# Expert stage of a two-block transformer: one-hot blocks one tile later, gate loads apart, gathered dots spread over the routings

## The reference

```python
s = jnp.einsum('chpd,hpnd->chpn', q, keys)
sv, si = lax.top_k(s, K)
cand = sv[:, :, 0, :, None] + sv[:, :, 1, None, :]
cidx = si[:, :, 0, :, None] * N_KEYS + si[:, :, 1, None, :]
top_s, sel = lax.top_k(cand.reshape(C, PEER_HEADS, K * K), K)
eidx = jnp.take_along_axis(cidx.reshape(...), sel, axis=-1)
g = jax.nn.softmax(top_s, axis=-1)
act = jax.nn.gelu(jnp.einsum('chkd,cd->chk', u_tab[eidx], xb), approximate=False)
return jnp.einsum('chk,chkd->cd', g * act, v_tab[eidx])
```

## Time and profile before

| | us |
|---|---|
| median of 3 runs (3055.06 to 3059.49) | 3056.42 |
| the profiled execution | 3056.66 |
| its span, first to last instruction | 3054.9 |
| TensorE busy in the span | 2918.0 |
| VectorE busy | 1802.1 |
| ScalarE busy | 996.8 |
| GpSimd busy | 999.0 |
| first pass, from the first product to the last gelu's end | 380.5 to 1068.4 |
| second pass, first to last product | 1068.4 to 1651.5 |

### The profile page before, as it was taken

One profiled execution on the slowest core, in us unless ns is written; L12 is line 12 of the kernel. 1 busy time (PEld: TensorE's weight loads), 2 busy tenths in 40 slices (PEclk: granted clock), 3 DMA queues, 4 the chain that ended last, 5 costly groups with the idle time before them and its releaser, 6 DMA issues. The chain is left out here.

```text
span 3054.9 us, 39382 instructions
## 1 busy us (share of the span) xinstructions
PE 2918.0 (96%) x15042; PEld 2591.1 (85%) x15042; DVE 1802.1 (59%) x3227; ACT 996.8 (33%) x1582; POOL 999.0 (33%) x611
## 2 busy tenths in 40 slices
PE   8887999999999799999999999999999899999998
PEld 7554799999999799999998787888788898778886
DVE  6785777888887677887884843331143455333311
ACT  4345233443434222222223223222223456332212
POOL 3201500111112432433332544444432344454442
PEclk9767999999999899999999999999999789999999
DMA  3101256786959988999983232233331000223332
GB/s 130 34 1 42 95 145 206 225 277 200 296 179 308 385 294 304 329 324 329 331 305 113 90 104 83 97 97 102 98 130 31 4 1 15 76 83 97 97 103 70
DMA packets 195745, 475.83 MB, mean 156 GB/s; under 512 B 17205, under 2 KB 104117, under 8 KB 193253
## 3 DMA queue, kind: packets, MB, share of 16 engines
q1 hardware_dynamic: 167764, 370.54, 37.0%
q0 software_dynamic: 27648, 100.68, 9.5%
q10 hardware_dynamic: 144, 2.10, 0.2%
HBM read 415.47 MB, written 56.62 MB: 155 GB/s over the span
## 5 line engine op out<-in xcount | busy, mean ns | idle before, releaser
L262 ACT ACTIVATE w_hi<-w 128x1024 fp32r<-128x1024 f32 (+2 forms) x485 | 506.6, 1046 | 1236.3 <-DVE ffn_gates L2119 324.4
L272 POOL TENSOR_TENSOR w_lo<-w,w_hi 128x1024 fp32r<-128x1024 f32 (+2 forms) x229 | 542.4, 2379 | 693.6 <-ACT w_hi L262 693.6
L272 DVE TENSOR_TENSOR w_lo<-w,w_hi 128x1024 fp32r<-128x1024 f32 x256 | 313.5, 1225 | 190.7 <-ACT w_hi L262 158.5
L307 PE MATMUL peer_psum<-xn_hi,w_hi 128*128 128x416 f32 x1024 | 369.0, 360 | 16.2 <-ACT peer_act_out L1627 16.2
L308 PE MATMUL peer_psum<-xn_lo,w_hi 128*128 128x416 f32 x1024 | 363.2, 355 | 0.0
L309 PE MATMUL peer_psum<-xn_hi,w_lo 128*128 128x416 f32 x1024 | 362.7, 354 | 0.0
L307 PE MATMUL peer_psum<-peer_w_hi,w_hi 128*128 128x416 f32 x1024 | 359.8, 351 | 2.1 <-DVE peer_w_lo L404 1.4
L308 PE MATMUL peer_psum<-peer_w_lo,w_hi 128*128 128x416 f32 x1024 | 358.9, 350 | 0.0
L309 PE MATMUL peer_psum<-peer_w_hi,w_lo 128*128 128x416 f32 x1024 | 358.9, 350 | 0.0
L1463 POOL DMA_INDIRECT peer_gathered<-in_peer_u,peer_chosen_here x96 | 141.5, 1474 | 623.0 <-DVEq L1710 496.0
L307 PE MATMUL ffn_psum<-ffn_hn_hi,w_hi 128*128 128x512 f32 x704 | 275.8, 392 | 10.4 <-DVE ffn_hn_lo L617 6.6
(11 more groups left out here) (417 smaller groups left out, 5724.5 us busy)
## 6 DMA issues: line engine op xcount, KB each, us to landing
w<-in_peer_uT SPq DMA_DIRECT2D x128, 512.0 KB
w<-in_peer_v SPq DMA_DIRECT2D x128, 512.0 KB
w<-in_f_w_gu SPq DMA_DIRECT2D x88, 512.0 KB
peer_act<-peer_act_out SPq DMA_DIRECT2D x128, 208.0 KB
peer_gate<-peer_gates_out SPq DMA_DIRECT2D x26, 1024.0 KB, 8.1
peer_gates<-peer_gate SPq DMA_DIRECT2D x16, 1664.0 KB, 9.6
peer_act_in<-peer_act SPq DMA_DIRECT2D x128, 208.0 KB
w<-in_f_w_down SPq DMA_DIRECT2D x32, 512.0 KB
```

Of the source, the lines that this page charges most:

```text
L262: act.activation(self.hi[:, x, 0:c], self.buf[:, x, 0:c], ACT.Copy).then_inc(self.rounded, 1)
L272: eng.tensor_tensor(self.lo[:, x, 0:c], self.buf[:, x, 0:c], self.hi[:, x, 0:c].bitcast(F32), ALU.subtract).then_inc(self.split, 1)
L307: pe.matmul(out, w[0], x[0], start=start, stop=False)
```

## The change

Five edits, all in `peer`:

- `block_tile` names the tile one later, so TensorE multiplies each block's one-hot matrices, ACT copies the gates out and SP stores them one tile later than before.
- SP loads the gates of q = 0 at c = 120 (`NK - 8`) instead of c = 122, still behind a wait for all gate stores. The gates of q = 1 are loaded behind the gelu of tile n = 4 in the second pass, not at c = 122.
- The tail makes one dot per tile.
- Each of the routings 1, 2 and 3 makes two dots, at two places in its chain.
- `EARLY` is 68: 48 in the blocks, 6 in the routings, 14 in the tail. So 28 dots are left to the second pass (20 before); `SHARES` goes from 23 to 31, and the adding of `peer_v` rows runs over n = 32 to 127 instead of 24 to 119.

```diff
-EARLY = 76
+EARLY = 68
@@
-                block_tile[START[r] + TURN + 1 + i] = b
+                block_tile[START[r] + TURN + 2 + i] = b
@@
-                    if c == NK - 6:
+                    if c == NK - 8:
                         for i in range(2):
                             sp.wait_ge(g_stored[i], 16 * len(range(i, n_slices, 2)))
-                        for q in range(2):
-                            load_gates(q)
+                        load_gates(0)
+                    if c == NK - 6:
                         for n in range(AS):
                             sp.wait_ge(a_stored[n], 16)
                             load_act(n)
@@
                     load_act(n)
+                    if n == AS + 1:
+                        load_gates(1)
@@
                         own.step(dve.max(svf[:, i, 8:16], rest[:, i, :]))
                         if i == 7:
                             weights()
+                            if r:
+                                early()
@@
                     own.wait()
                     weights()
+                    if r:
+                        early()
                     for h in range(PH):
                         own.step(dve.max(tops[:, h, 8:16], left[:, h, :]))
@@
                 while ahead[0] < NK - 2:
                     weights()
-                    for _ in range(2):
-                        early()
+                    early()
```

More of the change, by code:

```diff
@@ L1868, in _ @@
                     weights()
-                    for _ in range(2):
-                        early()
+                    early()
                 assert dotted_to[0] == EARLY
+                if EARLY == STEPS:
+                    own.wait()
+                    dve.nop().then_inc(dotted, 1)
                 for n in range(NK):
```

## The result

| | before | after |
|---|---|---|
| median, us | 3057.31 (15 runs, 3054.75 to 3073.16) | 3041.60 (15 runs, 3030.43 to 3053.39) |
| profiled execution | 3056.66 | 3043.8 |
| its span | 3054.9 | 3042.0 |

The ratio on record is 0.9936, 95% interval 0.9922 to 0.9951, so the kernel is faster by 0.64%. The two medians lie 15.7 us apart, which is 0.51%; they and the ratio weigh the scattered runs differently. The forecast was 30 us, and 3041.6 lies above its range. The direction was right, about half of the gain is missing.

A forecast was written before the change was run, and what follows sets the result against it. TensorE was taken as the bound, losing time only in the first pass. On the profiled execution, 3056.66 - 10.95 (first blocks) - 20.07 (tail) + 1.2 (second pass) = 3026.8, forecast as a 3027 us median, range 3020 to 3037.

The forecast's parts named there:

- The first blocks: First pass, r = 1, 2, 3: blocks one tile later remove TensorE's 1.92 us waits and half clock, -10.95 us.
- The 2.7 us of r = 3: TensorE's waits for ACT's copy of the gates: expected to stay, since the DMA engines there are 0.99 busy.
- The branch that I worked out under it: By the skill's line-rate rule, r = 3's waits are lateness from the first block and go: 2.7 us lower, 3024.
- The tail: Tiles 114 to 127, first pass: fewer gathers and split gate loads win back the whole loss, -20.07 us.
- the sign of 5: Sign of being right: no wait of ACT for a stored gelu over 5 us behind tile 114.
- The rival that the tail keeps a part: A gate load or the last gate store still delays stores: gives back 3 to 14 us, 3030 to 3041; chance 0.16.
- Dots in the routings: Two dots in each later routing, covered by DVE's waits for TensorE's pace: cost 0, without cover 9 us.
- Second pass: Eight more tiles carry a dot, so DVE loses time between gate loads: +1.2 us (0 to 4).
- the cost that I expected at n = 21: Second pass: the second gate load that makes DVE wait now falls among the dots; 1.2 us added for it.
- The rival that this pass turns to the bound: Second pass becomes bound by DVE at its 15 gate loads: 36 us, 3063, slower than before; chance 0.03.

The follow-up runs named there:

- s9: Kernel before with the dots and gate loads of the change, blocks not moved, and gate stores one tile earlier, at their block's tile: 3030.52 us, ratio 0.9909.
- s1: Changed kernel with SyncE storing a slice's gates at the tile of its second block instead of one tile behind it: 3029.71 us, ratio 0.9899.
- s7: Changed kernel without the move of the blocks (dots and gate loads only, stores where they were before): 3040.56 us, ratio 0.9942.
- s3: Kernel before with only the dots spread (EARLY, routings, tail), blocks and gate loads as before: 3046.61 us, ratio 0.9957.
- s12: The changed kernel with the early store profiled a second time, unedited: its three later block stretches took 406.9 us (407.0 in the first profile).
- s11: The changed kernel profiled a second time, unedited: its three later block stretches took 425.1 us (425.9 in the first profile).
- s5: Kernel before with one edit, SyncE's gate store one tile later; blocks, dots and gate loads untouched: 3170.53 us, ratio 1.0363.

## Why the prediction was right and wrong

**The first blocks, -10.95: wrong, and this is the step that failed.** The prediction says: "The blocks stand at nearly the same time after the turn as before (4.52 later, less the 3.65 lost), so ACT's copies and SP's stores meet the same traffic." The first half held (0.9 us later). The conclusion left out that SyncE's part is placed by its own loop, in tiles, and that loop keeps its pace from the weight ring: the store went 5.3 us later. The 3.65 us that TensorE lost at a first block had been the slack of that store. The wait and the half clock did go, as forecast; 12.4 us of waits at L1530 took their place, and the stretches became 3.09 us longer instead of 10.95 shorter. With the store a tile earlier they fall by 15.8 us: 10.2 by the move of the blocks (s9 to s1), and 5.6 by what s9 has over the kernel before (422.83 to 417.23), the early store above all, with which the copies' waits go (s7 to s9: 6.9).

**The 2.7 us of r = 3, left standing: wrong reason.** I had put them down to DMA engines 0.99 busy. In s1 they are gone with the engines 1.03 busy at 336 GB/s. They hang on the store as well: with it early they are gone in s9 too, where the blocks have not moved. The Trainium skill's rule that I set against the row ("DMA: Bandwidth & Descriptors", Specifications) is line rate from 512-byte pieces on. The branch that I worked out under it was right in that these waits are not a matter of the engines' room, and wrong in calling them lateness carried from the first block: s9 keeps the three waits there and has none for the copies. Nor do the runs show that such pieces reach the rate: with them the engines move 336 GB/s at 1.03, the tail 377 at 0.99.

**The tail, -20.07: the size right, the margin thinner than reckoned.** From the gelu of tile 114 to that of 127 it measured -20.07. The store behind the first gate load let ScalarE go on 10.35 us after its issue (1029.32 to 1039.67), where the prediction has some 10. The room that it reckons with is not there, though: it has 279 GB/s as the tail's traffic, and the window measured 377 at 0.99. From 994 to 1058 us the mean is 365; the gate stores, the gate load and three gelu loads come on top of the 279, and the sum had set only the gate load against it. The same slip stands in the reading of before, where "nothing but the tail's own traffic" leaves out the last gate store, issued at 990.08 and 18.3 us on its way. ScalarE still waits 3.71 and 4.50 us for stored gelus after, near the sign of 5 that I had set, and TensorE does not feel it, since it needs the gelu of two tiles back. That this was enough is in part luck. The rival that the tail keeps a part is refuted for this kernel; s3 shows it true when the gate loads stay where they were.

**Dots in the routings, 0: right at the turns, open elsewhere.** TensorE has no wait ahead of L1510 in any routing, and at the three turns VectorE still waits 1.75, 2.50 and 2.50 us for it. What the first dot of r = 1 may cost is in tiles 16 to 35. The seven profiles without it have 90.1 to 92.3 us there, before among them with 91.29. Of the seven with it four have 93.5 to 94.7 (s1, s12, s3, s7) and three 90.1 to 92.2 (s9, s11, after). So it cost 0.9 us or nothing in the changed kernel, and some 2 to 3 in others; why it differs is open.

**Second pass, +1.2: -0.74 measured**, too small a difference to tell from noise. Between its start and its end TensorE waits twice, 0.85 us at 1072.81, ahead of n = 3, and 0.27 at 1587.73. The first was 1.39 before and stands ahead of what the second gate load serves, and the cost that I expected at n = 21 is not there. The engines were 0.97 busy in the window that held the second gate load, and no wait followed. The rival that this pass turns to the bound fell.

**The sum.** Forecast -29.8 on the profiled execution, measured -12.9. Of the 16.9 missing, 14.0 are the block stretches, 4.1 the stages ahead and 2.6 tiles 0 to 35, less 1.9 in the second pass and 1.9 behind it. Between the two profiles of the changed kernel the last four differ by 2.7, 1.8, 3.6 and 0.8 us, so what is left of them beyond noise is small, and no run tells its cause.

## What to carry to other kernels

When a step is moved by a tile, move every engine's part of it in your head, and give each its own clock: which loop issues it, and what paces that loop. A wait that you take from the bound engine may be the slack of a transfer that another queue issues; compute for each double buffer when it is supplied and when it is asked for, before and after. Where the engine that waits for a buffer also feeds the ring that paces the supplier, lateness isn't made good from one round to the next: in s5 one tile's delay of the store cost 108 us, in 18 waits, not 5.

## What the runs showed of the hardware

- Full DMA engines and lost time are two things: 377 GB/s at 0.99 in a tail that loses nothing, 376 at 1.00 in the one before, which loses 20 us, though not in the window of that row. The difference is in when the one store that is waited for lands: 10.35 us from issue to release in the one, 22.6 in the other.
- The same wait has not the same price. In s9 three waits of 1.91, 1.91 and 1.92 us stand at the same place of three turns; the 3 us behind them had these clocks, and the stretch with the first is 1.5 us shorter (162.14 against 163.68):

```profile
568.90:571.90 3.00, 2.93 (x27) 2.92 (x28) 2.85 (x5) 2.03 (x3) 1.51 (x1) 1.00 0.39 150
731.10:734.10 3.00, 3.00 (x21) 2.93 (x22) 2.85 (x5) 2.14 (x3) 1.58 (x1) 0.60 0.45 165
894.80:897.80 3.00, 3.00 (x22) 2.92 (x23) 2.85 (x5) 2.09 (x3) 1.59 (x1) 0.63 0.42 164
```

- Issuing can take long itself. In s1, behind the twelve transfers of the token spread and two gate stores, one weight load keeps SyncE for 9.26 us, where 0.33 is the rule, and the gelu's store behind it is late by as much. ScalarE's wait at 526.47 and TensorE's 1.87 us hang on this; the 1.73 us at 516 are over before that store is issued. The load at this place took 9.84 us before and 3.67 in s9, which has no wait of TensorE there:

```profile
510.34 0.64 SPq L1436 DMA_DIRECT2D peer_gate<-peer_gates_out  x1
511.02 9.26 SPq L253 DMA_DIRECT2D w<-in_peer_uT  x1
520.33 0.43 SPq L1422 DMA_DIRECT2D peer_act<-peer_act_out  x1
...
526.47 0.52 ACT L1629 ACTIVATE peer_act_out<-peer_psum 128x416 f32<-128x416 f32 x1 [5.17 <-DMA peer_act<-peer_act_out]
...
527.13 0.43 PE L307 MATMUL peer_psum<-xn_hi,w_hi 128*128 128x416 f32 x1 [1.87 <-ACT peer_act_out L1629]
```
